# Gate table of a PEER layer: cell-by-cell additions by indirect transfers in place of one-hot matrix products

## What is computed

```python
s1 = einsum('tpd,pnd->tpn', q[:, :, 0], pk1)          # 128 keys
s2 = einsum('tpd,pnd->tpn', q[:, :, 1], pk2)          # 128 keys
v1, i1 = top_k(s1, 16);  v2, i2 = top_k(s2, 16)
cand = v1[..., :, None] + v2[..., None, :]            # 256 candidates
cidx = i1[..., :, None] * 128 + i2[..., None, :]
sc, pos = top_k(cand, 16);  e = take_along_axis(cidx, pos)
gate = softmax(sc)
act = gelu(einsum('tpkd,td->tpk', u_tab[e], h))
out = einsum('tpk,tpkd->td', gate * act, v_tab[e])
```

## Time and profile before

| | |
|---|---|
| median of 3 executions | 2340.7 us |
| the profiled execution | 2362.92 us |
| its span, first to last instruction | 2360.9 us |
| TensorE, share of the span | 94% |
| TensorE weight loads | 87% |
| VectorE | 64% |
| ScalarE | 37% |
| POOL | 17% |
| stage boundaries in the span | PEER from 606, first pass from 743, second pass from 1614, end 2361 |
| DRAM read / written | 272.64 MB / 76.28 MB |

### The profile page before, as it was taken

How to read it: one execution, slowest core, us unless ns; L and a number is a source line. 1 busy time by engine, 2 the same in 40 slices (tenths; PEclk the granted TensorE clock), 3 DMA queues, 4 the chain that set the end, 5 groups by cost and what they waited for, 6 DMA issues and landing times.

```text
span 2360.9 us, 42019 instructions
## 1 busy us (share of the span) xinstructions
PE 2221.2 (94%) x15400; PEld 2043.9 (87%) x15400; DVE 1516.0 (64%) x2464; ACT 865.3 (37%) x1367; POOL 412.7 (17%) x228
## 2 busy tenths in 40 slices
PE   5999998788799999999999999998899999999997
PEld 4888887678699999999999999997688888888886
DVE  6444445434698889987999999952345555554445
ACT  5434442332323434334444445542222222222222
POOL 2222222223234334541000000004101111100000
PEclk9999999899999999999999999998899999999998
DMA  5222220211122334433555455557467677656650
GB/s 204 82 99 95 91 83 27 90 62 50 52 75 89 130 131 134 136 122 116 180 180 179 176 180 180 180 189 247 151 204 239 233 241 258 232 192 204 198 175 38
DMA packets 170333, 349.74 MB, mean 148 GB/s; under 512 B 12416, under 2 KB 82208, under 8 KB 168096
## 3 DMA queue, kind: packets, MB, share of 16 engines
q1 hardware_dynamic: 164256, 332.17, 41.5%
q0 software_dynamic: 6016, 16.85, 2.2%
HBM read 272.64 MB, written 76.28 MB: 148 GB/s over the span
## 4 chain that ended last, share of the span: by engine, by line
PE 73%; DVE 20%; issue 3%; ACT 2%; POOL 1%; DVEq 0%; DMA 0%; ACTq 0%; SPq 0%; POOLq 0%
PE bank L785 21%; PE bank L787 21%; PE bank L786 21%; PE bank L1184 4%; DVE scr L1901 2%; DVE cand L1919 2%; DVE hit L1943 1%; PE bank L847 1%; DVE i L1900 1%; DVE i L1903 1%; DVE v L1902 1%; DVE v L1899 1%; DVE hit L1939 1%; DVE sel L1945 1%; DVE p L1903 1%
## 5 line engine op out<-in xcount | busy, mean ns | idle before, releaser
L785 PE MATMUL bank<-h_hi,u_hi 128*128 128x272 f32 x3136 | 924.6, 295 | 57.6 <-DVE h_lo L1683 27.9
L787 PE MATMUL bank<-h_hi,u_lo 128*128 128x272 f32 x3136 | 913.6, 291 | 0.0
L786 PE MATMUL bank<-h_lo,u_hi 128*128 128x272 f32 x3136 | 909.4, 290 | 0.0
L785 PEld LDWEIGHTS bank<-h_hi,u_hi 128*128 128x128 f32 x3136 | 597.8, 191 | 70.0 <-issue 35.0
L786 PEld LDWEIGHTS bank<-h_lo,u_hi 128*128 128x128 f32 x3136 | 597.9, 191 | 0.5
L787 PEld LDWEIGHTS bank<-h_hi,u_lo 128*128 128x128 f32 x3136 | 596.4, 190 | 0.0
L1537 ACT ACTIVATE u_hi<-wring 128x1024 fp32r<-128x1024 f32 x271 | 288.1, 1064 | 543.6 <-PE bank L787 463.8
L671 POOL TENSOR_TENSOR u_lo<-wring,u_hi 128x1024 fp32r<-128x1024 f32 x124 | 304.8, 2459 | 674.4 <-ACT u_hi L1271 401.0
L785 PE MATMUL bank<-w_hi,u_hi 128*128 128x512 f32 x1024 | 400.7, 391 | 9.3 <-issue 9.1
L787 PE MATMUL bank<-w_hi,u_lo 128*128 128x512 f32 x1024 | 400.6, 391 | 6.0 <-issue 6.0
L786 PE MATMUL bank<-w_lo,u_hi 128*128 128x512 f32 x1024 | 400.5, 391 | 4.1 <-issue 4.1
(11 more groups left out here) (251 smaller groups left out, 1893.1 us busy)
## 6 DMA issues: line engine op xcount, KB each, us to landing
wring<-in_u SPq DMA_DIRECT2D x128, 512.0 KB
wring<-in_v SPq DMA_DIRECT2D x128, 512.0 KB
scratch_act<-actb SPq DMA_DIRECT2D x128, 272.0 KB, 2.1
scratch_gates<-gst SPq DMA_DIRECT2D x16, 2048.0 KB, 7.3
a<-scratch_act SPq DMA_DIRECT2D x32, 1024.0 KB
g<-scratch_gates SPq DMA_DIRECT2D x32, 1024.0 KB
wring<-in_w_in SPq DMA_DIRECT2D x28, 512.0 KB, 3.4
wring<-in_w_x SPq DMA_DIRECT2D x24, 512.0 KB, 4.3
```

The costliest lines, as they stand in the source:

```text
L785: pe.matmul(out, whi, xhi, start=first, stop=False)
L786: pe.matmul(out, whi, xlo, start=False, stop=False)
L787: return pe.matmul(out, wlo, xhi, start=False, stop=last)
```

## The change

The table is cleared and then added to. In the front part SP writes 64 blocks of 512 KB of zeros (`clear`) between its weight loads, from a small zero tile that POOL sets at the start. VectorE finishes the selection of a head at once (`picked_cells`: 80 instead of 128 numbers per partition and step, all 5 token tiles together) and writes each picked cell's index to `gidx`. After every two heads ScalarE takes the exponentials (`gate_exp`) and VectorE the softmax (`gates_of`). POOL then issues, for each head, each of the four prompt token tiles and each of the 16 picks, one indirect transfer that adds 128 gates to 128 cells of the table: 8 x 4 x 16 = 512 transfers. Transfers of the same 16 picks wait for none of each other; a set of 16 waits for the set two before it and for the set of the previous head on the same tokens. POOL keeps 4 low halves; VectorE writes the other 124, ten inside each of heads 2 to 7. One-hot arrays, `gate_products`, the turning of `sel`, and `gst` are gone. The gates of a group are read as 2 KB rows, where they were read as 512 B rows. SP now waits for all scatters before it loads groups 0 and 1, both ahead of `first_group(last, d["v"], ...)`.

(Some argument lists are shortened.)

```diff
-U2_GROUPS = NCHUNK
-U3_GROUPS = 2
-U1_GROUPS = KEYS // GROUP - U2_GROUPS - U3_GROUPS
+U1_GROUPS = 1
+LOWS = 10
+EXP_AFTER = (2, 7, 12, 16)
+ZEROS = 64
...
+            def clear(n):
+                sp.dma_start(gate_zeros[n],
+                             zeros[:][:, None, :].to_broadcast([P, ZROW // ZW, ZW])).then_inc(zero_landed, 16)
...
             with sp.Fori(0, HEADS - 1) as i:
                 split(block_number(i, KR))
                 turn_weights(i + 1, KD, S_KD)
+                clear(i * 12 + 0)
...
+            for n in range(36, 40):
+                clear(n)
             with sp.Fori(0, PH // 2 - 1) as i:
                 for j in range(2):
                     for s in range(2):
                         b = 2 * j + s
                         sp.wait_ge(lo_ready, i * 4 + (FRONT + b + 1))
                         weights(b, d["w_pq"][i + 1, b])
+                        clear(i * 8 + (40 + 2 * b))
+                        clear(i * 8 + (40 + 2 * b + 1))
...
-            for p in range(2):
-                sp.wait_ge(g_stored[p], 16 + 16 * (NCHUNK // 2))
-            for j in range(GROUP):
-                sp.wait_ge(act_stored[j], 32)
-            sp.wait_ge(shuf_landed, 16 * 3 * KG)
-            load_group(0, 0)
+            for t in range(NT - 1):
+                sp.wait_ge(scattered[t], 16 * PH * TOPK)
+            for j in range(GROUP):
+                sp.wait_ge(act_stored[j], 16 + 16 * 2)
+            for p in range(2):
+                load_group(p, p)
             first_group(last, d["v"], 0, False)
-            load_group(1, 1)
...
+            def scatter(n):
+                p, t, k = n // ((NT - 1) * TOPK), n // TOPK % (NT - 1), n % TOPK
+                if n == 0:
+                    pool.wait_ge(zero_landed, 16 * ZEROS)
+                if k == 0:
+                    if t == 0 and p % 2 == 0:
+                        pool.wait_ge(pair_ready, p // 2 + 1)
+                    if p:
+                        pool.wait_ge(scattered[t], 16 * TOPK * p)
+                    before = n // TOPK - 2
+                    if before >= 0:
+                        pool.wait_ge(scattered[before % (NT - 1)], 16 * TOPK * (before // (NT - 1) + 1))
+                pool.indirect_dma_start(
+                    out=gate_cells, out_offset=bass.IndirectOffsetOnAxis(ap=gidx[:, p, t, k:k + 1], axis=0),
+                    in_=gate[:, p, t, k:k + 1], in_offset=None, compute_op=ALU.add,
+                ).then_inc(scattered[t], 16)
...
-            with pe.Fori(0, U2_GROUPS) as i:
-                for j in range(GROUP):
-                    first_products(i + U1_GROUPS, j, False)
-                    gate_products(i, j)
+            with pe.Fori(0, KEYS // GROUP - U1_GROUPS) as i:
+                for j in range(GROUP):
+                    first_products(i + U1_GROUPS, j, False)
...
+            def gate_exp(pair):
+                act.wait_ge(dif_ready, pair + 1)
+                mine = gexp[:, 2 * pair:2 * pair + 2].rearrange("p h t k -> p (h t k)")
+                act.activation(mine, mine, ACT.Exp).then_inc(gexp_ready, 1)
+            g = 0
+            for pair, end in enumerate(EXP_AFTER):
+                groups(g, end - g)
+                gate_exp(pair)
+                g = end
...
+            def picked_cells(i, j):
+                dve.tensor_scalar(rank[:, 0], of_p, 4, None, ALU.logical_shift_right)
+                dve.tensor_tensor(gexp[...], c16[:], c16[:, :, 0:1].to_broadcast([P, NT, TOPK]), ALU.subtract)
+                dve.tensor_copy(keyf[:], i16[:])
+                step.link(dve.tensor_scalar(rank[:, 1], of_p, TOPK - 1, None, ALU.bitwise_and))
+                step.link(dve.tensor_copy(rankf[:], rank[:]))
+                for s in range(2):
+                    step.link(dve.tensor_tensor(hit[:], rankf[:, s]..., iota[:, 0:TOPK]..., ALU.is_equal))
+                    step.link(dve.tensor_tensor(h4, h4, keyf[:, s]..., ALU.mult))
+                    step.link(dve.tensor_reduce(picks[:, s], hit[:], AX_X, ALU.add))
+                step.link(dve.scalar_tensor_tensor(out=ef..., in0=picks[:, 0], scalar=float(KEYS), in1=picks[:, 1], ...))
+                dve.tensor_copy(es..., ef[0:NG, NT - 1])
+                step.link(dve.scalar_tensor_tensor(out=at[:], in0=ef[:], scalar=float(ND), in1=tokf..., ...))
+                step.link(dve.tensor_copy(gidx..., at[:]))
...
+            for j in range(2):
+                top_head(0, j, lambda m: None)
+                picked_cells(0, j)
+            dve.sem_inc(dif_ready, 1)
+            with dve.Fori(0, PH // 2 - 1) as i:
+                top_head(i + 1, 0, low_of_head(0))
+                picked_cells(i + 1, 0)
+                dve.wait_ge(gexp_ready, i + 1)
+                gates_of(i)
+                top_head(i + 1, 1, low_of_head(1))
+                picked_cells(i + 1, 1)
+                dve.sem_inc(dif_ready, 1)
+            for n in range(late_low, late_low + 2 * GROUP):
+                low(n, n % RING)
+            dve.wait_ge(gexp_ready, PH // 2)
+            gates_of(PH // 2 - 1)
```

## The result

| | before | after |
|---|---|---|
| median of 4 runs each | 2341.5 us | 2568.4 us |
| lowest to highest | 2339.8 to 2343.3 | 2566.7 to 2569.1 |
| profiled execution | 2362.9 us | 2569.1 us |

After takes 1.097 times as long as before (95% interval 1.0956 to 1.0983), 227 us more. The forecast was 2261 us, in a range of 2220 to 2485: the sign was wrong, and the time lies 83 us above the range.

A forecast was written before the change was run, and what follows sets the result against it. TensorE was taken to bound the first pass. Removing 98.3 us there, then waiting for POOL's scatters, starts the second pass at 1534 instead of 1614.3; 2362.9 - 80 = 2283, times 0.9906 gives 2261 us, range 2220 to 2485.

The forecast's parts named there:

- The removal: First pass on TensorE: gate products, `sel` turning, idle time and its after-effect go, 98.3 us, all on the path.
- The zeros: Front part, SP's queue: 33.5 MB of zeros replace the old table stores; taken as 0, upper bound 10 us.
- VectorE level with TensorE: Heads 2 to 7: VectorE needs 60 us per head, TensorE 60.4 for ten tiles; 3 us lost over six heads.
- Rival 2: First pass: POOL's transfers hold up VectorE, 54 us more over six heads, first pass ends at 1570, total 2300; chance 0.12.
- POOL's start: First pass: POOL's scatters start at 819, once the first pair's gates are made after head 2.
- POOL's distance r: POOL's time from one transfer to the next: 1.35 us, between 1.25 and 1.62; 512 of them end at 1510.
- Rival 1: On POOL an addition costs more than a gather: 0.44 us extra, r = 1.79, total 2484; chance 0.25.
- What stands behind the last transfer: Between passes: 24 us kept from POOL's end at 1510, behind SP's wait, to the second pass at 1534.
- The second pass: 128 tiles at 5.44 us are 696; the pass lasts 730, its loss kept unchanged.
- My 34: Second pass: 34 us lost, nearly all while POOL issues gathers; kept, with 10 to 34 as bounds.
- Rival 3: A stream of small transfers starves the engines in the first pass: hundreds of us, 2700 or more; chance 0.08.
- The factor 0.9906: Whole kernel: median of executions over the profiled one, turning 2283 into 2261 us.

The follow-up runs named there:

- the kernel with sums: Changed kernel with plain instead of adding writes, VectorE adding earlier heads' gates for the same cell, first pair's gates finished inside head 2: 2237.7 us, 0.9555 of before.
- without transfers: Changed kernel with none of the 512 transfers, the gate table staying zero and SP waiting for the zeros only: 2235.7 us, 0.9545 of before.

## Why the prediction was wrong, point by point

**The removal: right.** 98.3 us were to come off TensorE and the first pass to end at 1516. Where nothing holds it up the second pass begins at 1516.9 (first product with `w_hi` in the kernel with sums) or 1514.8 (without transfers). The zeros cost nothing: the first pass begins at 743.1, as it did at 742.9.

**VectorE level with TensorE: right that it doesn't cost; the loss is 0 instead of 3.** VectorE is 267 of 301 us busy from 819 to 1120, its low halves wait 10 us there for ScalarE's high halves, and TensorE waits for none of them. Rival 2 was wrong.

**POOL's start: right.** Forecast 819, measured 819.59. It was there to be questioned, though: finished inside head 2, the gates of the first pair let POOL start 61.5 us earlier.

**POOL's distance r: wrong, and this is the step that failed.** The sum was 0.95 + 0.30 + 0.10 for VectorE's disturbance = 1.35; measured 1.958. The 0.30 is right to the hundredth (155.7 / 511), and so is the disturbance (mean 1.653 less undisturbed 1.55 = 0.10). The 0.95 for the transfer itself should have been 1.55. I priced a transfer that adds by a gather that doesn't. 0.60 x 512 = 307 us, and the last transfer came 310 us after the forecast's 1510. I had said that no row of before shows an adding scatter, and still took a value near the lower end; the "gather alone" row bore out only that the indirect form costs 0.95.

**Rival 1: the right mechanism in kind, too small.** It priced the addition at 0.44, to give 1.79 and 2484 us; the extra is 0.60: 0.95 + 0.30 + 0.60 + 0.10 = 1.95. Its reason, one descriptor list more for the cell that is read, fits only the price per cell, a quarter of the extra. And a bound of the range was a bound of one guess: no row limited the extra of an addition from above, so the range had no right to end at 2485. The Trainium skill (Collectives: The Full Stack, "Stop ④ — SDMA + CCE: where bytes move and the add happens") describes an AllReduce's addition as two reads and a write; that most of the 0.60 isn't paid by the cell (0.51 of it is left with 64 of the 128 cells) is what the runs add.

**What stands behind the last transfer: 4 us more.** From the last issue to the second pass I had 24 us; it is 27.9 (1820.00 to the first product with `w_hi`, at 1847.89). The sum left out the 3.2 us in which the last transfer lands and SP goes on. Then come 16.1 us to TensorE's return at 1839.28, 12.1 of them for the first `v` tile's load, and 8.6 for the last tile of the first pass, that had been held up with the rest. This tile takes 6.04 elsewhere. TensorE's clock had been granted at half while it stood idle (0.50 over 1514 to 1839), and for its first 24 products it still was:

```profile
1839.28:1844.66 5.38, 5.38 (x24) 5.38 (x25) 4.46 (x6) 3.77 (x7) 0.00 (x0) 0.50 0.79 255
1844.88:1847.89 3.01, 3.01 (x25) 3.01 (x25) 1.12 (x1) 0.40 (x1) 0.00 (x0) 1.00 0.15 59
```

Their starts are 0.23 us apart, those of the next 24 0.125: 2.6 us for the halved clock.

**The second pass: 27 us shorter than before, and I had kept that loss.** The second pass is 3072 products. From the start of the first to that of the last they take 696.2 us here (1847.89 to 2544.05), as much as in the kernel without transfers and in the one with sums, and 723.4 before (1614.17 to 2337.61). So before lost 27 us, and after nothing. My 34 was a misreading: the 730 us also held some 7 us behind the last product, that every kernel has. The 27 are idle times of "issue" between 1630 and 1668 us, 19 in sum, and products that ran 0.43 us apart instead of 0.23 while the granted clock was at half. The window of the kernel with sums, over the stretch in which POOL issues the same gathers, answers to the last one of the earlier trace rows:

```profile
1520.00:1545.00 25.00, 25.00 (x112) 20.72 (x111) 11.72 (x15) 6.93 (x9) 19.51 (x19) 1.00 0.84 313
```

POOL is 19.5 of 25 us busy with them and TensorE 25 of 25. So the gathers do not stop TensorE, and neither do 512 transfers beside the first pass (Rival 3 was wrong). What the engine waited for in the profiled execution of before stays open.

**The factor 0.9906: wrong too.** The profiled execution of before was 21 us above its median, that of after only 0.7 above its own. I kept the loss of the second pass and took the 21 us off as well. That the other executions of before hadn't most of this loss is likely from that, but no trace of one shows it.

The sum closes in both forms. Profiled: 2283 + 310 + 4 - 27 = 2570; measured 2569.1. Median: 2261 + 310 + 4 - 27 + 21 = 2569; measured 2568.4. The three small terms cancel nearly, so the 307 us between forecast and result are, in size, the 310 of r.

## What to carry to other kernels

Price an instruction by its own form: an indirect transfer that adds cost the issuing engine 1.6 times one that writes, while both carry half a kilobyte, and this kernel with 512 of them was bound by the issuing engine and not by the DMA engines, which were 26% busy while all else stood still. When work is taken off the busiest engine, write down for the engine that gets it: start, count x distance, end, and the moment at which somebody waits for that end; here a distance of 1.32 was free and each 0.01 more cost 5 us. And where a transfer adds only because a few addresses meet, let an engine with idle time add beforehand and let the transfer overwrite in order.

## What the runs showed of the hardware

- POOL's time to issue an indirect transfer of single 4-byte cells: 0.96 us for 128 cells written, 0.89 for 64; with an addition 1.55, 1.40 and 1.31 for 128, 64 and 32; 0.30 between two of them. The last one landed 3.0 us after its issue began with an addition, 2.1 without.
- POOL's queue carried 16 packets and one for each cell for an adding transfer (144, 80, 48), and 32 for a plain one of 128 or 64 cells.
- A transfer that POOL begins within the first 1.1 us of a low half of VectorE (two inputs, 1024 elements, 1.22 us) ends a fixed time after it, 0.83 us plain and 1.43 adding for 128 cells, so it is lengthened by up to 1.0 us, the less the later it begins; one begun before that operation isn't lengthened.
- 28 pairwise comparisons of 16 with 16 cells for four token tiles cost VectorE 109 us in all, 1.22 us for each operation on 1024 elements.
- While TensorE stood idle for 329 us its granted clock went to half, 1.2 instead of 2.4 GHz (0.50 over 1514 to 1839), and stayed there until 1844.87, TensorE having run without a gap since its return at 1839.28. Its products of 272 columns started 0.23 us apart up to then and 0.125 after, which cost 2.6 us.
- In the second pass of before, products of 512 columns started 0.43 us apart at the halved clock and 0.23 at the full one.
